# Transposes in attention, even column blocks in the value stage, and an earlier gelu in a hybrid-attention and PEER layer

## What is computed

```python
p = softmax(q @ k.T * scale + bias)            # per head; 28 such calls in all
o = p @ v_head                                 # times a gate in the 6 gated heads

q = (x @ wq).reshape(b, s, 8, 2, 128)          # 8 query heads
sc = einsum('bshcd,hckd->bshck', q, subkeys)
# 16 best of each half, then the 16 best of their 256 sums: expert numbers and g = softmax(best)
act = gelu(einsum('td,tkd->tk', x, u[experts]))     # 128 experts a token
y = einsum('tk,tkd->td', g * act, v[experts])
h = h + y
h = h + sigmoid(rmsnorm(h) @ ple_gate) * (p @ ple_proj)
```

## Time and profile before

| | us |
|---|---|
| median of 3 runs | 1847.0 (1846.05 to 1850.13) |
| the profiled execution | 1844.21 |
| its span | 1842.2 |
| TensorE busy (matmul) | 1320.0 (72%) |
| VectorE busy | 1448.2 (79%) |
| ScalarE busy | 769.3 (42%) |
| GpSimd busy | 792.5 (43%) |

### The profile page before, as it was taken

One profiled execution on the slowest core, in us unless ns is written; L12 is line 12 of the kernel. 1 busy time (PEld: TensorE's weight loads), 2 busy tenths in 40 slices (PEclk: granted clock), 3 DMA queues, 4 the chain that ended last, 5 costly groups with the idle time before them and its releaser, 6 DMA issues. The chain is left out here.

```text
span 1842.2 us, 24073 instructions
## 1 busy us (share of the span) xinstructions
PE 1320.0 (72%) x7651; PEld 1161.5 (63%) x7651; DVE 1448.2 (79%) x1972; ACT 769.3 (42%) x1349; POOL 792.5 (43%) x839
## 2 busy tenths in 40 slices
PE   7999999999984671000111222299999999999997
PEld 6999999988973450000111111278888888888886
DVE  5334555564478799999999999889999999999855
ACT  4324445554210022000566666683333333333554
POOL 1100000000054355555555555288777777777303
PEclk9999999999998786555555555599999999999999
DMA  7974444456599999999999999919999999999952
GB/s 241 294 225 138 138 138 138 138 199 231 175 403 411 409 412 408 405 403 414 415 405 413 408 403 411 420 43 374 372 361 367 364 365 365 360 366 367 338 187 110
DMA packets 172277, 577.15 MB, mean 313 GB/s; under 512 B 14805, under 2 KB 88870, under 8 KB 138289
## 3 DMA queue, kind: packets, MB, share of 16 engines
q0 software_dynamic: 58544, 367.16, 50.4%
q1 hardware_dynamic: 113664, 209.10, 32.8%
HBM read 571.99 MB, written 7.36 MB: 314 GB/s over the span
## 5 line engine op out<-in xcount | busy, mean ns | idle before, releaser
L1505 DVE SCALAR_TENSOR_TENSOR rows<-rows,banks 128x2048 f32<-128x2048 f32 x232 | 519.9, 2279 | 17.7 <-DMA rows<-peer_u_dram,expert 16.3
L707 POOL DMA_INDIRECT rows<-peer_u_dram,expert x232 | 220.4, 950 | 422.0 <-DVE rows L1505 167.4
L751 POOL DMA_INDIRECT vrow<-peer_v_dram,vidx x224 | 280.2, 1251 | 113.2 <-DVE hres L1609 63.9
L2050 PE MATMUL banks<-hot,hot 128*128 128x128 f32 x512 | 103.3, 367 | 237.2 <-ACT hot L1090 233.2
L2050 PEld LDWEIGHTS banks<-hot,hot 128*128 128x128 f32 x512 | 89.1, 263 | 251.6 <-issue 178.5
L805 ACT CAST whi<-raw 128x2048 fp32r<-128x2048 f32 x80 | 152.2, 1904 | 174.7 <-PE banks L1788 97.0
L1609 DVE SCALAR_TENSOR_TENSOR hres<-vrow,slot_coef,hres 128x704 f32<-128x704 f32 x224 | 213.0, 951 | 4.1 <-DMA vrow<-peer_v_dram,vidx 4.1
L2094 PE MATMUL banks<-vlo,chi 128*128 128x192 f32 x762 | 192.1, 387 | 0.2 <-DVE vlo L1623 0.2
L1623 DVE TENSOR_TENSOR vlo<-vraw,vhi 128x1216 fp32r<-128x1216 f32 x128 | 181.3, 1416 | 0.5 <-ACT vhi L1138 0.5
L1270 DVE TENSOR_TENSOR wlo<-raw,whi 128x2048 fp32r<-128x2048 f32 x46 | 106.0, 2305 | 92.5 <-ACT whi L805 91.4
L1133 ACT CAST chi<-spread 128x256 fp32r (+1 forms) x128 | 52.0, 406 | 296.9 <-PE banks L2094 289.8
(11 more groups left out here) (289 smaller groups left out, 2972.1 us busy)
## 6 DMA issues: line engine op xcount, KB each, us to landing
vraw<-peer_v_dram SPq DMA_DIRECT2D x128, 672.0 KB
raw<-w_in_dram SPq DMA_DIRECT2D x48, 1024.0 KB, 5.5
raw<-w_out_dram SPq DMA_DIRECT2D x16, 1024.0 KB, 5.3
wqraw<-peer_wq_dram SPq DMA_DIRECT2D x32, 512.0 KB, 16.1
raw<-ple_gate_dram SPq DMA_DIRECT2D x16, 1024.0 KB, 5.6
rows<-peer_u_dram,expert POOLq DMA_INDIRECT x232
vrow<-peer_v_dram,vidx POOLq DMA_INDIRECT x224
bias_by_distance<-bias_of_heads POOLq DMA_DIRECT2D x1, 3072.0 KB, 12.6
```

What stands on the lines that cost most here:

```text
L707: pool.indirect_dma_start(dst[:, :], None, peer_u[0], bass.IndirectOffsetOnAxis(ap=expert[b][:, k:k + 1], axis=0))\
L751: pool.indirect_dma_start(vrow[j][:, :], None, pieces, bass.IndirectOffsetOnAxis(ap=idx[:, j % TT, j // TT:j // TT + 1], axis=0))\
L1505: dve.scalar_tensor_tensor(out=r[:, :], in0=r[:, :], scalar=1.0, in1=xps[tt][:, :], op0=ALU.mult, op1=ALU.mult, accum_out=dots[b][:, k:k + ...
L2050: last = pe.matmul(bank[SPREAD_BANK[m]][:, a * P:(a + 1) * P], hot2[tt][m][:, a, :], hot1[tt][m][:, a, :], start=True, stop=True)
```

## The change

Three parts.

- **Attention.** VectorE scales the probabilities in `pb` in place (`normalise`), in two instructions of 128 and 256 columns (7 and 15 on compressed keys), instead of scaling two identities; TensorE transposes them with its transpose instruction. The wait of VectorE for the transposes two calls earlier goes with the `diag` buffers.
- **Value stage.** There are no plain columns any more: 1376 columns are dense, all of them split, in blocks of 460, 458 and 458, and 672 are gathered. The table comes in two packed arrays, the gathered columns and the dense ones, so the row numbers need no factor. The product, the copy, the transposes and the additions for the plain columns go. Buffers are placed anew: chi in the place of earlier row buffers (so ScalarE waits for `pp_out` before the first), clo behind the ring of vraw.
- **ScalarE's order.** `gelu(0, 1)` (step 1) moves ahead of `take_head(5)`, and `take_head(6)` moves behind `gelu(1, 0)` (step 2).

```diff
-VCOL = 512
-VGATH = 704
-VPLAIN = 128
+VGATH = 672
 VDENSE = D - VGATH
-VSPLIT = VDENSE - VPLAIN
-PIECE = 64
+VCOLS = [460, 458, 458]
...
-            vview = peer_v[0].rearrange("(c q) d -> q c d", q=P)
+            vview = v_dense.rearrange("(c q) d -> q c d", q=P)
...
-                ps.did(pool.tensor_scalar(row4[:, :], bidxf[:, 1, :], float(D // PIECE), None, ALU.mult))
-                ps.wait_apart()
-                ps.did(pool.tensor_copy(slot_row[:, slots], row4[:, :]))
+                ps.did(pool.tensor_copy(slot_row[:, slots], bidxf[:, 1, :]))
...
-                    pool.indirect_dma_start(vrow[j][:, :], None, pieces,
+                    pool.indirect_dma_start(vrow[j][:, :], None, v_gathered,
...
             step_scores(3)
+            gelu(0, 1)
             take_head(5)
-            gelu(0, 1)
-            take_head(6)
             route_exp(1, 1, False)
             step_scores(4)
             gelu(1, 0)
+            take_head(6)
             take_head(7)
...
+                if peeled and r == 0:
+                    act.wait_ge(pp_out, 16)
...
-                act.copy(vhi[r % 2][:, :], vraw[r % VRING][:, VPLAIN:]).then_inc(vhi_ready, 1)
+                act.copy(vhi[r % 2][:, :], vraw[r % VRING][:, :]).then_inc(vhi_ready, 1)
...
-            act.wait_ge(v_used, TT * (NKEYS - VROWS // TT) + 1)
-            act.wait_ge(vplain_mm, 1)
-            act.copy(vplain[:, :], bank[6][:, 0:SEQ]).then_inc(vplain_sb, 1)
...
-                if c >= 2:
-                    dve.wait_ge(s_pt, c - 1)
-                for tt in range(TT):
-                    dve.tensor_scalar(diag[c % 2][:, tt, :], ident[:, :], r[:, tt:tt + 1], None, ALU.mult)\
-                        .then_inc(s_diag, 1)
+                w, w0 = (RLEN, P) if kind == "full" else (NCMP0 + NCMP, NCMP0)
+                for tt, cols in ((0, slice(0, w0)), (1, slice(w0, w))):
+                    dve.tensor_scalar(pb[c % 3][:, cols], pb[c % 3][:, cols], r[:, tt:tt + 1], None, ALU.mult)\
+                        .then_inc(s_norm, 1)
...
-                    pe.matmul(dst[:, 0:P], pr_[:, 0:P], dg[:, 0, :], start=True, stop=True)
-                    pe.matmul(dst[:, P:2 * P], pr_[:, P:2 * P], dg[:, 1, :], start=True, stop=True)
-                    last = pe.matmul(dst[:, 2 * P:RLEN], pr_[:, 2 * P:RLEN], dg[:, 1, :], start=True, stop=True)
+                    for n in range(3):
+                        last = pe.transpose(dst[:, n * P:(n + 1) * P], pr_[:, n * P:(n + 1) * P], ident[:, :])
...
-                v_plain(i, r, first=first)
...
-            v_plain(V_TURNS - 1, r, stop=True).then_inc(vplain_mm, 1)
...
-                if b == 0:
-                    pe.wait_ge(vplain_sb, 1)
-                    for tt in range(TT):
-                        last = pe.transpose(bank[7][:, tt * P:(tt + 1) * P], vplain[:, tt * P:(tt + 1) * P], ident[:, :])
-                    last.then_inc(vplain_tr, 1)
```

82 lines of the change are left out of this document (32 added, 50 removed).

## The result

The changed kernel takes **1837.8 us** (median of 20 runs, 1831.7 to 1852.2); the kernel before takes 1848.3 beside it (1843.0 to 1851.6). So there are two errors to find: 7.3 us between two profiled executions (12.0 gained, 19.3 forecast), and 2.8 us in the way from a profiled execution to the median (5.6 us here, 2.8 put in).

The account below looks back on a forecast made before the run. Bounds: TensorE in projection with attention and in the value stage; the hand-over to VectorE's row work between. From 1844.21 us, - 19.8 - 0.5 - 9.0 + 10 gives 1824.9, plus 2.8 to the median: 1828 us, range 1820 to 1836.

Parts of the forecast that it names:

- Attention: Attention calls: single true transposes replace two-instruction products with a scaled identity, saving 9.0 us, bounds 0 to 9.
- Rival E: Attention: the transposes save nothing because the spacing of pairs hides it; + 9 us, 1837 us; chance 0.05.
- Hand-over: From query weights to row fetches: late query blocks delay the 65th fetch and step 3's gelu; + 10 us, bounds - 4 to + 15.
- Rival B: Hand-over costs nothing: query weights come as fast, or the 65th fetch isn't held; 1816 us; chance 0.20.
- Value stage: Value stage: TensorE's step falls from 3.867 to 3.71 us, gaining 19.8 us in 128 steps, bounds 4 to 27.
- Each product carries some 15 ns besides: Value stage: each TensorE product costs its columns plus 15 ns, 206 ns for 459 columns, 3.71 us a step.
- Both run behind deep buffers: Value stage: the argument against DMA or VectorE becoming the bound, with buffers 4 dense and 8 gathered.
- ScalarE is busy 173 of 440 us and GpSimd 330: covered: Value stage: ScalarE and GpSimd have room enough, so neither was given a cost.
- Rival C: Value stage gains only 2 to 11 us, DMA or VectorE bounding it at 3.78 to 3.85 us; 1840 us; chance 0.15.
- Rival D: Value stage: slower transfers from packed tables, at 350 GB/s a 3.98 us step, + 14 us, 1861 us; chance 0.08.
- The end: End of the value stage: copy, transposes and additions for the plain columns go, four waits fewer, 0.5 us saved.
- Sum: Whole kernel: - 19.8 - 0.5 - 9.0 + 10 = - 19.3 us against the profiled execution, giving 1824.9 us.

Follow-up runs that it names:

- half_order: The changed kernel with only the gelu of step 1 moved ahead of query head 5, head 6 left in its old place; 1834.4 us, ratio 0.9943.
- after_split: The changed kernel with vlo in two pieces of 688 columns and the second addition of gathered rows between them; 1832.0 us, ratio 0.9926.
- light_gather: The changed kernel with ScalarE's earlier order, each gather fetching 336 columns instead of 672, read twice; 1824.3 us, ratio 0.9889.
- 640-column variant: The changed kernel with ScalarE's earlier order, 640 gathered columns and dense blocks of 470, 470 and 468; 1860.8 us, ratio 1.0088.

## Why the prediction was wrong, point by point

- **Attention: right.** 9.0 us forecast; the first fetch came 9.35 us earlier, and the part alone gave 0.56%, 10 us. All of it was on the path. Rival E fell.
- **Hand-over: right, in size and in way.** + 10 forecast, + 8.96 in the profiles, 10.7 by the ratios (7.2 with the order alone). The blocks of query weights came 10.5 to 11.5 us apart up to the last, whose product ended at 691.3 us, 700.7 on the clock of before (forecast 699.5); the 65th fetch was used at 707.3 on that clock (forecast 705.7), after a wait of 10.2 us; the coefficients of step 3 at 724.2 (forecast 724.5), after a wait of 0.8 us for the gelu (forecast 2.5). `half_order` cost as much by another wait, VectorE's for scores, which the forecast's account didn't have. Rival B (nothing lost) fell.
- **Value stage: the step that failed**, 12.8 us instead of 19.8, in two places.
  - "Each product carries some 15 ns besides": this term was too small. It is 17.4 in this stage: 208.5 instead of 206 ns a product, 3.755 instead of 3.71 us a step, 0.045 x 128 = **5.8 us**, most of the 7.3 that the profiled execution fell short. I took the 15 ns from the gate stage, though the products of the value stage itself carried 22, and explained those away by their uneven blocks. The cuts show that unevenness costs nothing (512, 432, 432 is as quick as 460, 458, 458). It was within my bounds, and I took the value too near to the good end. Why it is 17.4 and not 14 or 15 stays open. The formula of the Trainium skill, TensorE: Matmul & The Clock Gate, section Back-to-back issue gap (3.49 us a step), was further off still.
  - "Both run behind deep buffers", with 2% of room in DMA and 3% in VectorE as the doubts. The remaining 1.2 us of the profiled execution are stalls; TensorE stands for 1.35 us after 1300, where the chain shows the late row. That term I had put at nothing: "ScalarE is busy 173 of 440 us and GpSimd 330: covered". I counted how vlo grows on VectorE (1416 to 1586 ns, 1562 by my rate) and not what a longer vlo does to GpSimd, whose gathers went from 1256 to 1527 ns. `after_split` shortens them again and is 0.24% quicker than the changed kernel by the ratios, 4.4 us, at the edge of what the intervals tell. Full transfers have a part in it: `light_gather` has gathers of 1634 ns, longer than any other with 672 columns, and not one late row, with half of the gathered bytes. Rival C had the right sign (less gained in the value stage), and DMA or VectorE as a bound at 3.78 us or more a step, which didn't appear. Rival D fell; the packed tables change nothing that can be told.
- **The end**: + 1.2 us where - 0.5 was forecast. ScalarE waits 2.9 us there for the first weights of the gate; no run took this apart, and from the value stage's last product to the end it is 108.0 to 110.5 us in the twenty profiles, 109.3 and 109.4 in two that keep the old value stage, so it may be no more than scatter.
- **Sum**: - 19.3 + 5.8 + 1.2 + 1.7 - 0.35 - 1.0 = - 12.0 us (the value stage's two errors, the end, the attention, the hand-over), and 2.8 more to the median, whose cause is open. For late gathers as the cause of the slowest runs (up to 1852 us) speak `after_split`'s narrower runs and the 640-column variant, whose second profile, 15 us slower, showed them; against them, `light_gather`, which has no late row and runs over 12 us. None of the runs of the changed kernel over 1834.5 us was profiled.

## What to carry to other kernels

Price a product by products of the same stage, even if they are less regular than others of the profile, and keep the gap between the two rows in the forecast. When an instruction on VectorE grows, look at what GpSimd does beside it: the mean of GpSimd's own instructions shows what it is held up, and near to no waits for free buffers are a warning (17.1 of 430 us with 640 columns). In a stretch where the DMA engines are full, ask first whether a change would leave them empty; a stall that only moves from one wait to another under full transfers was worth nothing here.

## What was not expected of the hardware

- GpSimd's gather of 128 rows takes 0.94 us by itself. Held up, it ended some 0.82 us behind the end of a VectorE instruction, be it vlo in either form, an addition or clo: 1.2 to 2.4 us where it started during a vlo of 1.59 us, 2.7 to 3.2 where it started in the addition ahead of it. With vlo in pieces of 0.87 us it took 1.05 on average with 672 columns, and still 1.45 with 704. With 640 columns one program fell into steps of 3.88 us with few stalls in one execution, and of 3.84 with 50 us of waits in another.
- What a product of TensorE takes besides columns / 2.4 at full clock isn't a constant: 14 ns in the gate stage, and in the value stage 16.0, 17.0 to 17.5, 17.8, 20.0 and 20.2, with 20.0 and 17.8 in two executions of one program. It goes neither by the cut nor by the bytes, and halving vlo changed it with 448 columns (20.0 to 16.0) but not with 459 (17.4). The cause is open.
